# Hosted modulation: weight rows scaled and summed on VectorE, partitions added on TensorE once per 1024 columns

## The reference, cut to what matters

```
m = silu(cvec) @ ada_w[l] + ada_b[l]            # 1024 x 6144 weights per layer l, for c and for c_ctx
shift_m, scale_m, gate_m, shift_f, scale_f, gate_f = split(m, 6)
u = rms_norm(h, g) * (1 + scale) + shift
h = h + gate * rms_norm(mixer(u), g')
```

## Time and profile before

| | us |
|---|---|
| median of 3 runs | 1958.94 (1957.56 to 1959.04) |
| profiled execution, its own time | 1959.78 |
| its span | 1958.0 |
| TensorE busy | 1853.6 |
| VectorE busy | 961.0 |
| ScalarE busy | 846.7 |

### The profile page before, as it was taken

The page is one execution under the profiler, slowest core; times in us unless marked ns, Lnnn a source line. Parts: engine busy times, 40 slices in busy tenths (PEclk is TensorE's granted clock), DMA queues, the critical chain, the costliest instruction groups (busy, mean ns, idle before and its releaser), DMA issues.

```text
span 1958.0 us, 27046 instructions
## 1 busy us (share of the span) xinstructions
PE 1853.6 (95%) x10365; PEld 1517.7 (78%) x10365; DVE 961.0 (49%) x1373; ACT 846.7 (43%) x1217; POOL 108.7 (6%) x176
## 2 busy tenths in 40 slices
PE   5999999999999999999998999799999988999997
PEld 2766766767668877788887887699879975779986
DVE  1533323323247633344437566466665576665554
ACT  2423233233345522233326455555554544644453
POOL 3011111101100011100000000000001000000000
PEclk9999999999999999999999999899999998999999
DMA  9444544434347465331322223256645543545663
GB/s 312 130 144 127 154 137 134 148 123 149 126 141 257 128 208 172 96 106 65 129 86 91 82 76 97 83 175 187 197 152 177 164 140 109 160 151 175 181 194 104
DMA packets 151295, 282.43 MB, mean 144 GB/s; under 512 B 13027, under 2 KB 78683, under 8 KB 151072
## 3 DMA queue, kind: packets, MB, share of 16 engines
q1 hardware_dynamic: 133344, 220.54, 36.0%
q0 software_dynamic: 17856, 60.56, 9.6%
HBM read 276.83 MB, written 4.23 MB: 144 GB/s over the span
## 4 chain that ended last, share of the span: by engine, by line
PE 83%; DVE 7%; ACT 4%; DMA 3%; issue 2%; POOL 0%; SPq 0%; ACTq 0%; DVEq 0%
PE ps L559 24%; PE ps L560 23%; PE ps L561 23%; PE ps L812 4%; PE ps L604 2%; DVE wl L2203 2%; DMA raw<-in_ada_w 2%; ACT wh L1502 1%; PE ps L805 1%; DMA arena<-in_ada_w 1%; DMA arena<-in_norm_g 1%; PE ps L1107 1%; PE ps L1088 1%; PE ps L699 1%; PE ps L712 1%
## 5 line engine op out<-in xcount | busy, mean ns | idle before, releaser
L2203 DVE TENSOR_TENSOR wl<-raw,wh 128x1024 fp32r<-128x1024 f32 (+1 forms) x388 | 454.6, 1182 | 643.8 <-ACT wh L1502 641.6
L1502 ACT ACTIVATE wh<-raw 128x1024 fp32r<-128x1024 f32 (+1 forms) x388 | 393.0, 1022 | 734.8 <-PE ps L561 715.4
L559 PE MATMUL ps<-uh,wh 128*128 128x256 f32 (+1 forms) x1216 | 382.3, 314 | 7.3 <-DVE spare L2225 7.3
L560 PE MATMUL ps<-ul,wh 128*128 128x256 f32 (+1 forms) x1216 | 379.9, 312 | 0.0
L561 PE MATMUL ps<-uh,wl 128*128 128x256 f32 (+1 forms) x1216 | 379.8, 312 | 0.0
L559 PE MATMUL ps<-wh,uh 128*128 128x512 f32 (+2 forms) x960 | 364.5, 380 | 13.3 <-issue 8.8
L560 PE MATMUL ps<-wl,uh 128*128 128x512 f32 (+2 forms) x960 | 356.4, 371 | 0.0
L561 PE MATMUL ps<-wh,ul 128*128 128x512 f32 (+2 forms) x960 | 355.4, 370 | 0.0
L559 PEld LDWEIGHTS ps<-uh,wh 128*128 128x128 f32 x1216 | 233.4, 192 | 26.2 <-issue 10.8
L561 PEld LDWEIGHTS ps<-uh,wl 128*128 128x128 f32 x1216 | 233.3, 192 | 13.0
L560 PEld LDWEIGHTS ps<-ul,wh 128*128 128x128 f32 x1216 | 233.3, 192 | 12.4
(11 more groups left out here) (295 smaller groups left out, 1513.3 us busy)
## 6 DMA issues: line engine op xcount, KB each, us to landing
raw<-in_ffn_w_up SPq DMA_DIRECT2D x176, 256.0 KB
arena<-in_ada_w POOLq DMA_DIRECT2D x80, 512.0 KB, 4.8
raw<-in_w_in SPq DMA_DIRECT2D x60, 512.0 KB
raw<-in_ret_w_in SPq DMA_DIRECT2D x48, 512.0 KB
raw<-in_ffn_w_down SPq DMA_DIRECT2D x40, 512.0 KB
raw<-in_ret_w_out SPq DMA_DIRECT2D x32, 512.0 KB
raw<-in_w_up SPq DMA_DIRECT2D x32, 512.0 KB
raw<-in_w_down SPq DMA_DIRECT2D x32, 512.0 KB
```

The lines of the kernel that those rows point to most:

```text
L559: pe.matmul(o, lh, rh, start=first, stop=False)
L560: pe.matmul(o, lh, rl, start=False, stop=False)
L1502: T.mark(act.activation(wh[:, j, 0:size], raw[:, j, 0:size], ACT.Copy), hi_done)
L2203: T.mark(vec.tensor_tensor(wl[:, j, 0:size], raw[:, j, 0:size], wh[:, j, 0:size], ALU.subtract), lo_done)
```

## The change

The twenty hosted tiles become ten vectors of 1024 columns (`MODS`), four of them gates (`GATES`, the indices 0, 3, 6 and 9). A unit is now 128 weight rows x 1024 columns, eight to a vector, and still 512 KB. VectorE multiplies the unit by the condition vector's value of its row, a per-partition scalar, and adds it to a running sum, once for each of the two condition vectors (`sum_unit`). After eight units TensorE adds the 128 partitions of the two sums with eight matmuls of 256 columns (`add_rows`), ScalarE copies the result out (`keep_mods`), TensorE turns it (`turn_mods`), VectorE adds the bias (`take_mods`). A gate is turned back into rows for its store (`turn_gate`, `keep_gate`).

In retention one unit stands behind each of VectorE's splits in the steps d = 1 to 14 (d = 4h + step; `sum_slot`), and TensorE's three pieces stand in the odd steps from d = 3 on, behind slots 0, 1 and 2. In the FFN the units stand in i = 1 to 6, TensorE's pieces in i = 3, 5 and 7, the last gate's turn in i = 8. The bias rows and their loads are gone; the loads and stores on GpSimd's queue are in a new order.

```diff
-            def ada_unit(n, u, bank):
-                m = (n - 4) * SLOTS + u
-                pe.wait_ge(ada_loaded[m % 2], 16 * (m // 2 + 1))
-                ada_matmuls(n, u, aring[:, m % 2, :], bank)
...
+            def add_rows(q, half):
+                pe.wait_ge(ada_summed, 8 * q + 8)
+                for c in range(2):
+                    for x in range(4):
+                        mm = pe.matmul(ps[32 * x:32 * x + 32, half + 3, 0:256], select[:, c, :], sums[q][:, c, x * 256:(x + 1) * 256],
+                                       start=c == 0, stop=c == 1)
+                mm.then_inc(ada_added, 1)
+
+            def turn_mods(q, half):
+                pe.wait_ge(mods_kept, q + 1)
+                for x in range(2):
+                    mm = pe.matmul(ps[:, half + 2, 8 * x:8 * x + 8], adas[:, 0, x * P:(x + 1) * P], rows8, start=True, stop=True)
+                mm.then_inc(ada_turned, 1)
+
+            def turn_gate(q, half):
+                pe.wait_ge(ada_taken, 5 + q)
+                pe.transpose(ps[0:16, half + 3, 256:256 + P], gate_cols, ident[:, :]).then_inc(gate_turned, 1)
+
+            def host_mods(d, j, half):
+                if d > 2 and d % 2:
+                    q = (d - 3) // 2
+                    if j == 0:
+                        add_rows(q, half)
+                    elif j == 1:
+                        turn_mods(q, half)
+                    elif j == 2 and q in GATES:
+                        turn_gate(q, half)
...
+            def sum_unit(u):
+                q, k = divmod(u, KD)
+                vec.wait_ge(ada_loaded[u % 2], 16 * (u // 2 + 1))
+                if k == 0 and q:
+                    vec.wait_ge(ada_added, q)
+                T.settle()
+                for c in range(2):
+                    o, w = sums[q][:, c, :], aring[:, u % 2, :]
+                    if k:
+                        ins = vec.scalar_tensor_tensor(out=o, in0=w, scalar=c32[:, k, c:c + 1], in1=o, op0=ALU.mult, op1=ALU.add)
+                    else:
+                        ins = vec.tensor_scalar(o, w, c32[:, k, c:c + 1], None, ALU.mult)
+                    T.mark(ins, (vec_own, ada_summed)[c])
+
+            def sum_slot(d, j):
+                if 0 < d < 15:
+                    sum_unit(4 * (d - 1) + j)
...
                     split(units=range(3, 4))
+                    sum_slot(d, 3)
                 else:
                     split()
                 rotate(h)
...
                 split(units=range(3, 4))
+                sum_slot(d + 1, 3)
                 hb = step_full()
                 T.mark(vec.tensor_copy(vres[:, 2:4, :], ps[:, hb + 2:hb + 4, :]), vec_own)
                 close()
...
+                elif i < 8:
+                    u = 56 + 4 * (i - 1)
+                    split(units=range(0, 1))
+                    if i in (3, 5, 7):
+                        split(units=range(1, 3))
+                        take_mods(6 + i // 2, main)
+                        if i < 7:
+                            sum_unit(u)
+                            sum_unit(u + 1)
+                    else:
+                        sum_unit(u)
+                        split(units=range(1, 2))
+                        sum_unit(u + 1)
+                        split(units=range(2, 3))
+                    if i < 7:
+                        sum_unit(u + 2)
+                    split(units=range(3, 4))
+                    if i < 7:
+                        sum_unit(u + 3)
...
+            for u in range(8 * len(MODS)):
+                load_mods(u)
+                if u % 8 == 4 and u // 8 - 1 in GATES:
+                    store_gate(u // 8 - 1)
```

More of the change, by code:

```diff
@@ L606, in ada_matmuls @@
                 mm.then_inc(ada_used, 1)
-            def ada_unit(n, u, bank):
-                m = (n - 4) * SLOTS + u
-                pe.wait_ge(ada_loaded[m % 2], 16 * (m // 2 + 1))
-                ada_matmuls(n, u, aring[:, m % 2, :], bank)
             def turn_ada(n, bank):
                 pe.wait_ge(ada_kept, n + 1)
[L619 to L624, removed]
+                for x in range(2):
+                    mm = pe.matmul(ps[:, bank, 4 * x:4 * x + 4], adas[:, n % 2, x * P:(x + 1) * P], pick,
+                                   start=True, stop=True)
                 mm.then_inc(ada_turned, 1)
@@ L1705, in _ @@
                 T.mark(act.activation(vres[:, 0:2, :], ps[:, hb:hb + 2, :], ACT.Copy), act_evac)
-                split(units=range(0, 3))
-                keep_ada(n + 2, side + 3)
-                split(units=range(3, 4))
+                split()
                 silu_gate(sgf)
@@ L1833, in _ @@
                     split()
-                elif i < 6:
-                    split(units=range(0, 3))
-                    keep_ada(18 + i, (side if i % 2 == 0 else main) + 3)
-                    split(units=range(3, 4))
+                elif i in (3, 5, 7):
+                    split(units=range(0, 2))
+                    keep_mods(6 + i // 2, main)
+                    split(units=range(2, 4))
+                elif i == 8:
+                    split(units=range(0, 2))
+                    keep_gate(9, side)
+                    split(units=range(2, 4))
                 elif i < 10:
@@ L2507, in _ @@
                 split(units=range(0, 1))
-                take_ada(n + 1, side + 2)
                 masks(h)
+                sum_slot(d + 2, 0)
                 vec.wait_ge(scored, 2 * h + 1)
@@ L2513, in _ @@
                 split(units=range(1, 2))
+                sum_slot(d + 2, 1)
                 vec.wait_ge(scored, 2 * h + 2)
                 decay((3,), side)
-                split(units=range(2, 4))
+                split(units=range(2, 3))
+                sum_slot(d + 2, 2)
+                split(units=range(3, 4))
+                sum_slot(d + 2, 3)
                 step_full()
@@ L2523, in _ @@
                 ahead(range(0, 1))
-                take_ada(n + 2, main + 2)
+                sum_slot(d + 3, 0)
                 gate(4 * h, main)
                 ahead(range(1, 2))
+                take_mods(2 * h, main)
+                sum_slot(d + 3, 1)
                 gate(4 * h + 1, main)
-                ahead(range(2, 4))
+                ahead(range(2, 3))
+                sum_slot(d + 3, 2)
+                ahead(range(3, 4))
+                sum_slot(d + 3, 3)
             step_full()
```

209 lines of the change are left out of this document (100 added, 109 removed).

## The result

The changed kernel takes 1940.71 us (median of 4 runs, 1938.88 to 1942.23); the kernel before, beside it, 1958.99 (1957.56 to 1959.41). The ratio is 0.9908, with a 95% interval of 0.989 to 0.9925: 0.9% faster, 18.3 us. The forecast was 1938. The profiled execution has a span of 1938.8 us and a mean granted clock of 0.979, against 1958.0 and 0.983.

The account below looks back on a forecast made before the run. TensorE, busy 95% of the span, was taken as the bound. Work alone 44.7 us less, minus 7.5, 7.2, 4.2, 1.8 and 3.0 in waits and clock, left 21.0 less: 1938 us, with 1921 to 1954 for 8 in 10.

Parts of the forecast that it names:

- Work alone: Whole change: TensorE work and load waits removed, 61.6 us, less new work of 16.9, gives 44.7 us less.
- Given back: Retention and first FFN: new TensorE waits on VectorE and half clock return 7.5, 7.2, 4.2, 1.8 and 3.0 us.
- rotation, 3 waits: Heads 1 to 3, before y's second turn: a unit ahead of the rotation delays TensorE 2.5 us each, 7.5.
- half clock behind them: After the three 3.8 us rotation waits: TensorE's clock falls to half, 2.4 us apiece, 7.2, bounds 0 and 9.6.
- v's copy, 4 waits: End of each head's second step: 2.5 us more ahead of the copy against 1.4 of cover, 4 x 1.05 = 4.2.
- backward gate: First step of heads 1 to 3: TensorE work that hid the gate leaves, 0.6 us wait each, 1.8.
- closes after SiLU: After the two SiLU steps: the unit's sum stays hidden with 0.3 us left, cost 0.
- FFN waits: First FFN, i = 5 and i = 7: TensorE waits 1.2 to 1.5 us each for late evacuations, 3.0.
- The second rival: First FFN: slower load landings make the two waits 2.6 to 4.0 us with half clock, 1945 to 1948 us; chance 0.20.
- the prediction's own sign: First FFN: waits at i = 5 and 7 above 2.5 us were named as showing the forecast wrong.
- The first (the cover holds better, 1929): Retention and FFN: 3.8 us waits bring no clock fall, loads land in 4 us, 14.5 comes back; chance 0.22.
- The slow one: VectorE becomes the bound: a unit takes 3.5 us instead of 2.5, costing 34 in all, 1972 us; chance 0.12.

Follow-up runs that it names:

- v's copy first: Changed kernel with the unit's sum behind slot 3 of each head's second step moved behind v's copy and its PSUM release: 1935.97 us, ratio 0.9874.
- unit behind slot 2: Changed kernel with slot 3's unit summed ahead of slot 3's split in the first step of heads 1 to 3: 1929.36 us, again 1925.24.
- two areas in the FFN: Changed kernel with a second running-sum area for the ninth vector and one unit behind each FFN split instead of three in a row: 1934.64 us.
- units of no length: Changed kernel where seven of eight units multiply and add only 8 of 1024 columns, so most sums are left out: 1914.88 us, ratio 0.9769.
- all three: Changed kernel with v's copy first, slot 3's unit ahead of its split in heads 1 to 3, and the FFN's second running sum: 1918.11 us, again 1921.75.
- longer units: Changed kernel with one more VectorE pass over 512 columns, 0.69 us, in each of the 80 units: 1963.03 us, ratio 1.0014.
- unit behind the rotation: Changed kernel with slot 3's unit summed behind the rotation in first steps of heads 1 to 3, TensorE's pieces one slot later: 1924.79 us.
- the same, with v and FFN: Changed kernel with the unit behind the rotation, v's copy ahead of its unit, and the FFN's second running sum: 1916.02 us, ratio 0.9778.
- The ninth kernel: The kernel "the same, with v and FFN", with the rotation also ahead of slot 3's split on VectorE in all four heads: 1912.31 us, ratio 0.9757.

## Why the prediction came out right, step by step

The stretch that the change touches can be measured alone, from TensorE's wait near 82 us to the turn of rows that opens the next block (1036.55 before):

| kernel | from | to | shorter than before by |
|---|---|---|---|
| before | 82.85 | 1036.55 | |
| the change | 81.09 | 1014.15 | 20.6 |
| the change, again | 83.22 | 1016.58 | 20.3 |
| v's copy first | 84.05 | 1010.67 | 27.1 |
| unit behind slot 2 | 82.66 | 1004.91 | 31.5 |
| unit behind slot 2, again | 82.38 | 1002.07 | 34.0 |
| two areas in the FFN | 82.78 | 1010.59 | 25.9 |
| units of no length | 81.30 | 988.33 | 46.7 |
| all three | 82.85 | 993.46 | 43.1 |
| all three, again | 82.40 | 996.27 | 39.8 |
| longer units | 81.67 | 1035.63 | -0.3 |
| unit behind the rotation | 82.00 | 1001.86 | 33.8 |
| the same, with v and FFN | 83.60 | 991.40 | 45.9 |

The ninth kernel has no wait near 82 us to start from. From its first turn of q, at 84.89, it takes 902.05 us to the same end, and the kernel of the last row 902.21. The three waits of 1.30 in this part are gone, but this profile waits 2.02 us at the FFN's start and not 0.63, and is at half clock for 3.4 us at 516 and at 629.

What follows 1036.55 took 921.45 us before, 924.65 in the first profile of the change and 921.82 in the second. So the first profiles differ by 20.6 in the stretch and 1.8 ahead of it, less 3.2 behind it, 19.2 in all. Over all 14 profiles the part behind took 921.4 to 924.7, so the 18.3 us of the medians and the 20.6 of the stretch can't be told apart.

**Work alone: the mis-sized term.** Forecast 44.7. Units of no length give 46.7, with waits left over in them of 3 x (1.77 - 1.30) and 4 x 0.52, 3.5 us; so the work alone is worth about 50.2. The step that was too low is the sum of the pieces. Turns cost 0.36 and not 0.44, and a gate's turn back 0.02 and not 0.25: 10 x 0.08 + 4 x 0.23 = 1.7 of the 5.5.

The other 3.8 lie mostly in retention. From the wait near 82 to the first FFN's start (663.02 before, 630.37 here) this kernel takes 31.1 us less, 34.6 with its own waits; from there on, 15.6 less. My pieces add up to 30.4 and 14.2. One cause can be read from rows: I had priced a unit by its own start to start, with a break of 0.2 only where nothing else stood in the slot. Here is the second turn of q and k with two units in the kernel before, and the same turn alone in the change, from the last matmul of a row to the first of the next:

```profile
95.92 0.39 PE L561 MATMUL ps<-wh,ul 128*128 128x512 f32 x1
...
98.11 0.50 PE L559 MATMUL ps<-wh,uh 128*128 128x512 f32 x1
```

```profile
92.79 0.39 PE L571 MATMUL ps<-wh,ul 128*128 128x512 f32 x1
...
93.81 0.48 PE L569 MATMUL ps<-wh,uh 128*128 128x512 f32 x1
```

2.19 less 1.02 is 1.17 for the two units, where the sum has 1.00. So a piece beside other small work had its break too. Eleven slots of retention are of this kind (a turn of q, k or y with one or two units), 0.17 each, 1.9 us. About 2 us of the 5.5 stay open, and 0.8 more, because one term was too high: the 1.0 for waits for loads in retention was an estimate, and the trace of before has one such wait there, 0.19 us at 509.83.

**Given back.** Forecast 23.7; 50.2 - 20.6 = 29.6 measured. By terms:

| term | forecast | measured |
|---|---|---|
| rotation, 3 waits | 7.5 | 3 x (3.88 - 1.30) = 7.7 |
| half clock behind them | 7.2 | 3.4 + 3.4 + 6.8 = 13.6 us at half, 1.9 of it inside the waits: at most 5.9 |
| v's copy, 4 waits | 4.2 | 4 x 1.05 = 4.2 |
| backward gate | 1.8 (3 places) | 0.55 + 0.55 + 0.53 + 0.53 = 2.2 (4 places) |
| closes after SiLU | 0 | 0 |
| FFN waits | 3.0 | 2.62 + 1.66 = 4.3, and 3.4 us at half clock, 1.7 |
| start of the first FFN | not seen | 1.75 - 0.63 = 1.1, and 3.4 us at half clock, 1.7 |

The measured column adds to 28.8 with the clock at its bound (half of the time at half clock, where TensorE works); 0.8 isn't found. The bound is about right where it can be measured alone: from one adding of rows to the next the FFN takes 814.36 - 769.12 = 45.24 us with two areas and 817.94 - 769.40 = 48.54 in the change, which is the wait of 1.66 and 1.64 for the 3.4 us at half clock. That a half clock can begin inside a wait shows in head 3, where TensorE is idle and the clock already at half (columns of the earlier trace rows):

```profile
448.70:450.40 1.70, 0.00 (x0) 0.00 (x0) 1.50 (x6) 0.00 (x0) 0.00 (x0) 0.50 0.86 311
```

The waits in VectorE's order were right to a tenth of a microsecond, because each is a sum of rows: the unit's passes were in the profile of before with their form, and the cover of each place with its start and end. The fourth gate wait is in the step after the last head's projections, at 551.47, where the same attend stands without the head's next step; I had looked at heads 1 to 3 only. The FFN waits were too low by 1.3 (2.62 and 1.66, where I had 1.2 to 1.5 each). The load isn't the reason: the third unit of the triple waits 2.53 us, and its load lands 4.8 us after its issue (732.87), as I had taken it. What the chain by hand had too short is the evacuation: it ends 14.9 us after its step in i = 3 and 13.3 in i = 4, where I had 14 and 12 (counted as there, from ScalarE's split of the last slot, at 734.24 and 756.00, to the end of the multiply, 749.13 and 769.34).

**The clock.** That waits of 3.88 us cost a half clock each held in every profile: 12 of 12 in the four with such waits, and 3 of 3 behind 4.23 in the kernel with longer units. The forecast had it from one wait of 3.80, a thin basis that turned out to carry. The second rival's line ("2.6 to 4.0, the length from which the rows show the clock at half") is not a line at all: of twelve waits of 1.85 to 1.87 us five have a half clock behind them, three and one in the two profiles of one schedule, none and one in those of another. One FFN wait, 2.62, did bring a fall in the first profile of the change, and 1.99 brought one in the second. The first is at the lower end of the rival's range, and by the prediction's own sign (a wait there above 2.5 us) a piece of that rival came true; its price was 1.6 us and not 7 to 10.

**The loads.** I kept 4.8 us from the trace. The longer rows land in 4.3 (median of 80), with GpSimd's issue of one at 0.53 us where it had been 0.71; no run here parts the rows' length from the other traffic. By the Trainium skill, "DMA: Bandwidth & Descriptors" (Anatomy of one DMA), 2.0 us plus the bytes at 436 GB/s, an estimate for this size is 3.2 us. The measurement is nearer to the trace of before, and it decides.

**The rivals.** The first (the cover holds better, 1929) fell with its condition: the clock did fall behind the waits of 3.88. The slow one's condition was that a unit be longer than its row says or wait for its load; units took 2.48 as forecast, and in retention none waits for a load. Its price was right in sum: the forecast had the gain eaten up from 0.6 us a unit on, and with 0.69 more the kernel is 0.14% slower than before. That price is the more useful finding: the change stands 0.6 to 0.7 us a unit from being worth nothing.

In sum, the mechanism was right and the number owes something to two errors that cancel: 5.5 us too little for the work, 5.9 too little for what comes back.

## What to carry to other kernels

When work moves from the bounding engine to one with room, its time is not the question, but what stands behind it in that engine's order: here VectorE's units of 2.48 us cost nothing where they stood behind the instruction that frees a PSUM bank, and ahead of it their length less the cover there: 2.58 us at the rotation, which had no cover, 1.05 at v's copy, nothing at the closes after SiLU. So list each place where the bounding engine waits for the other, put new work behind the release, and count the work that leaves as cover that is lost. The change as given gains 0.9%; with a few calls moved and one more area for the sums it gains 2.4%, of which 5 us are a wait that the kernel before had too.

## What the runs showed of the hardware

TensorE's granted clock, by the idle time just before, between 60 and 870 us of all profiles: after waits of 1.30 us never a half clock; after 1.85 to 1.87 in 5 of 12; after 2.26 or 2.27, at the attend near 516 to 555 us, in 3 of 14; after the waits of 1.36 to 2.62 in the first FFN and at its start in 12 of 22; after 3.88 to 4.25 in 15 of 15, and after 6.30 and 6.67 in both. In 11 of the 15 the clock fell before the wait had ended. A wait's length alone doesn't decide it in between, and neither does the program, since it differs between two executions of one kernel. A fall lasts 3.4 or 6.8 us. What else decides stays open.

The start of the first FFN is of two kinds in all kernels, whatever was edited: 0.63 us in six of 14 profiles (that of before among them), 1.75 to 2.20 in eight. In all eight ScalarE's last split ahead of it had waited 2.8 to 3.2 us for a weight load, in the six it had not; why the load lands late was not settled.
